# Output sum of the second token tile in three pieces, and two projections copied out of PSUM bank by bank

## The reference, cut to what matters

```python
def hybrid_layer(x, ...):
    h = rms_norm(x, g_pre) * (1 + scale) + shift
    qkv_dn, z_dn, beta_logit, a_logit, qkv_mb, z_mb, merge_logit = split(h @ w_in)
    qkv_dn = silu(causal_depthwise_conv(qkv_dn, conv_w))      # dq, dk, dv in the kernel
    ...                                                       # gated delta rule, 4 heads of 128
    o_mb = moba_attention(q_mb, k_mb, v_mb)                   # bq, bk, bv in the kernel
    ...
    mixed = (gate_dn * y_dn + gate_mb * y_mb) @ w_out         # "out" in the kernel
    return x + gate * rms_norm(mixed, g_post)
```

## Time and profile before

| | us |
|---|---|
| median of 3 runs | 895.02 |
| profiled execution, its own time | 895.32 |
| its span (first to last instruction) | 893.5 |
| PE busy | 884.4 |
| DVE busy | 652.2 |
| ACT busy | 498.4 |

### The profile page before, as it was taken

How to read it: one execution, slowest core, us unless ns; L and a number is a source line. 1 busy time by engine, 2 the same in 40 slices (tenths; PEclk the granted TensorE clock), 3 DMA queues, 4 the chain that set the end, 5 groups by cost and what they waited for, 6 DMA issues and landing times.

```text
span 893.5 us, 13339 instructions
## 1 busy us (share of the span) xinstructions
PE 884.4 (99%) x5610; PEld 756.6 (85%) x5610; DVE 652.2 (73%) x790; ACT 498.4 (56%) x676; POOL 31.1 (3%) x25
## 2 busy tenths in 40 slices
PE   8999999999999999999999999999999999999997
PEld 7889888888888888888888888888879998888885
DVE  6999656569777767699567977777668895556655
ACT  6875556465444454766566544445558774366624
POOL 0000000000000000000000000000000083000000
PEclk9999999999999999999999999999999999999999
DMA  9644444466666664544336666666336344324431
GB/s 357 275 146 179 149 142 142 142 247 222 241 227 240 230 241 167 202 157 161 120 142 255 228 240 230 239 239 235 142 132 244 120 142 143 116 101 155 137 129 47
DMA packets 24155, 165.40 MB, mean 185 GB/s; under 512 B 2688, under 2 KB 2944, under 8 KB 4896
## 3 DMA queue, kind: packets, MB, share of 16 engines
q1 hardware_dynamic: 22608, 159.73, 48.9%
q0 software_dynamic: 1056, 4.34, 1.3%
q10 hardware_dynamic: 432, 0.49, 0.2%
HBM read 163.50 MB, written 1.05 MB: 184 GB/s over the span
## 4 chain that ended last, share of the span: by engine, by line
PE 91%; DVE 5%; ACT 2%; DMA 1%; issue 1%; DVEq 0%; SPq 0%; ACTq 0%
PE acc L633 30%; PE lin L594 11%; PE lin L615 6%; PE lin L622 6%; PE lin L599 6%; PE lin L616 6%; PE lin L573 3%; PE lin L581 3%; PE lin L574 3%; DVE w_lo L1889 2%; PE acc L841 1%; PE acc L725 1%; PE acc L726 1%; DVE arena L2342 1%; PE acc L735 1%; PE lin L678 1%
## 5 line engine op out<-in xcount | busy, mean ns | idle before, releaser
L1889 DVE TENSOR_TENSOR w_lo<-raw,w_hi 128x2048 fp32r<-128x2048 f32 x137 | 318.4, 2336 | 127.7 <-ACT w_hi L1384 127.1
L1384 ACT CAST w_hi<-raw 128x2048 fp32r<-128x2048 f32 x137 | 259.6, 1907 | 138.0 <-DMA raw<-in_weights 86.0
L633 PE MATMUL acc<-w_hi,f_hi 128*128 128x512 f32 x288 | 113.1, 393 | 0.0
L633 PE MATMUL acc<-w_hi,f_lo 128*128 128x512 f32 x288 | 112.4, 390 | 0.0
L615 PE MATMUL lin<-w_hi,h_both 128*128 128x512 f32 x272 | 109.4, 402 | 0.2
L594 PE MATMUL lin<-h_both,w_hi 128*128 128x512 f32 x448 | 106.7, 390 | 0.0
L616 PE MATMUL lin<-w_hi,h_both 128*128 128x512 f32 x272 | 106.3, 391 | 0.0
L594 PEld LDWEIGHTS lin<-h_both,w_hi 128*128 128x128 f32 x448 | 83.2, 188 | 16.7
L633 PE MATMUL acc<-w_lo,f_hi 128*128 128x512 f32 x288 | 78.9, 389 | 0.0
L622 PE MATMUL lin<-w_lo,h_both 128*128 128x512 f32 x272 | 68.1, 390 | 0.2 <-DVE w_lo L1889 0.2
L573 PE MATMUL lin<-h_both,w_hi 128*128 128x256 f32 x272 | 67.3, 287 | 0.0
(11 more groups left out here) (372 smaller groups left out, 1225.7 us busy)
## 6 DMA issues: line engine op xcount, KB each, us to landing
raw<-in_weights SPq DMA_DIRECT2D x149, 1024.0 KB, 4.8
rowbuf<-in_rows POOLq DMA_DIRECT2D x6, 512.0 KB, 4.0
x<-in_x_in SPq DMA_DIRECT2D x2, 512.0 KB, 4.5
raw<-in_weights SPq DMA_DIRECT2D x2, 512.0 KB, 7.3
arena<-in_const_even POOLq DMA_DIRECT2D x1, 1024.0 KB, 11.6
out<-x SPq DMA_DIRECT2D x3, 256.0 KB, 2.1
cst<-in_const SPq DMA_DIRECT2D x1, 580.0 KB, 10.4
out<-x ACTq DMA_DIRECT2D x1, 256.0 KB, 2.1
```

The costliest lines, as they stand in the source:

```text
L633: return pe.matmul(acc[:, at:at + 512], part_of(2 * j + k)[i][:, t * P:(t + 1) * P], w[:, k * 1024 + c * 512:k * 1024 + (c + 1) * 512], st ...
L1384: act.copy(w_hi[:, o % SPLIT, :], raw[:, j % RAW, :]).then_inc(hi_done, 1)
L1889: dve.tensor_tensor(w_lo[:, j % RAW, :], r, hi.bitcast(F32), ALU.subtract).then_inc(tile_split, 1)
```

## The change

1. The second token tile of `out` is summed in three pieces instead of two: columns 0 to 511 in the third bank of `acc`, 512 to 767 in the fourth, 768 to 1023 in the first bank of the pair that `y2a` has left. For the last two pieces each matmul has 256 columns. Squares, gain, update of x and stores follow the pieces; the last two stores have 128 KB each, one from SP, the last from ACT.
2. `dv` is copied out in two copies of 512 columns. The first stands in ACT's list behind the exponentials and ahead of `conv_silu` of q, and waits for the first tile of `dv`; the second stands where the whole copy stood.
3. `bk` is copied out in two copies of 512 columns. The wait for `qg_ready` moves from behind the cast of the second `bv` tile to ahead of it; both copies stand behind the cast.

```diff
+        def last_piece(i):
+            at, width = ((0, 512), (512, 256), (768, 256))[i]
+            return (acc[:, D + at:D + at + width] if i < 2 else pair("y2a")[:, 0:width]), at, width
...
+            for i in range(2):
+                _, at, width = last_piece(i)
+                sp.wait_ge(x_done, done + 3 + i)
+                sp.dma_start(out[0, P:T, at:at + width], x[:, 1, at:at + width]).then_inc(s_out, 16)
+            sp.wait_ge(s_out, 16 * 5)
...
+            def second_tile(n, piece):
+                o, at, width = last_piece(piece)
+                hi = high_tile(FIRST["out"] + n)
+                for k in range(2):
+                    w = slice(k * D + at, k * D + at + width)
+                    for i in range(2):
+                        pe.matmul(o, chunk(2 * n + k)[i][:, P:T], hi[:, w], start=n == 0 and k == 0 and i == 0, stop=False)
+                lo = low_tile(FIRST["out"] + n)
+                for k in range(2):
+                    w = slice(k * D + at, k * D + at + width)
+                    mm = pe.matmul(o, chunk(2 * n + k)[0][:, P:T], lo[:, w], start=False, stop=n == 3 and k == 1)
+                return mm
...
+            for piece in range(3):
+                for n in range(2, 4):
+                    mm = second_tile(n, piece)
+                    if piece == 2:
                         mm.then_inc(tile_used, 1)
+                if piece < 2:
+                    mm.then_inc(acc_done, 1)
...
+            def half_out(name, i, dst):
+                act.wait_ge(tile_used, ORDINAL[FIRST[name] + i] + 1)
+                ins = act.copy(dst[:, i * 512:(i + 1) * 512], pair(name)[:, i * 512:(i + 1) * 512])
+                if i == 1:
+                    ins.then_inc(freed(name), 1)
...
             act.activation(srow(4), srow(2), ACT.Exp).then_inc(erow_ready, 1)
+            half_out("dv", 0, at("pre", 1024, 2048))
             conv_silu(S_AT["q"])
...
             load_exp()
-            copy_out("dv", at("pre", 1024, 2048), splits=False)
+            half_out("dv", 1, at("pre", 1024, 2048))
             split_until(LAST["dv"] + 1)
...
                 if l == 2:
+                    act.wait_ge(qg_ready, 1)
                     split_until(LAST["bq"] + 4)
-                    act.wait_ge(qg_ready, 1)
-                    copy_out("bk", at("bk"), splits=False)
+                    half_out("bk", 0, at("bk"))
+                    half_out("bk", 1, at("bk"))
...
+                after(ss_ready)
+                piece_gain(0)
+                after(ss_ready)
+                link(dve.tensor_scalar(stat[:, 5:6], stat[:, 2:3], stat[:, 3:4], EPS * D, ALU.add, ALU.add))
+                piece_gain(1)
+                after(ss_ready)
+                dve.tensor_tensor(stat[:, 17:18], stat[:, 5:6], stat[:, 4:5], ALU.add).then_inc(ms_ready, 1)
+                piece_gain(2)
+                root_of(1)
+                for i in range(3):
+                    _, at, width = last_piece(i)
+                    part = x[:, 1, at:at + width]
+                    dve.scalar_tensor_tensor(part, arena[:, 6144 + D + at:6144 + D + at + width], stat[:, 9:10], part,
+                                             ALU.mult, ALU.add).then_inc(x_done, 1)
```

More of the change, by code:

```diff
@@ L499, in _ @@
                 sp.dma_start(raw[:, n % RAW, :], weights[n]).then_inc(loaded[n % RAW], 16)
[L500 to L507, removed]
+            done = 4 * (len(SUMS) - 1)
+            for c in range(2):
+                sp.wait_ge(x_done, done + c + 1)
+                sp.dma_start(out[0, 0:P, c * 512:(c + 1) * 512], x[:, 0, c * 512:(c + 1) * 512]).then_inc(s_out, 16)
+            for i in range(2):
[3 more added lines that the diff above has]
+            sp.wait_ge(s_out, 16 * 5)
         @block.gpsimd
@@ L1344, in _ @@
                     mm.then_inc(half_done, 1)
[L1346 to L1349, removed]
-                        mm.then_inc(tile_used, 1)
[L1351 to L1361, removed]
+            def second_tile(n, piece):
[10 more added lines that the diff above has]
+                return mm
+            for n in range(2):
+                row_products(FIRST["out"] + n, n, 0, range(2), chunk, n == 0, False)
+            after(mix_ready)
+            transposes(["y2b"], y_mix, 4)
+            for n in range(2):
+                for piece in range(3):
+                    mm = second_tile(n, piece)
+                mm.then_inc(tile_used, 1)
+            for c in range(2):
+                for n in range(2, 4):
+                    mm = row_products(FIRST["out"] + n, n, 0, (c,), chunk, False, n == 3)
+                mm.then_inc(acc_done, 1)
+            for piece in range(3):
+                for n in range(2, 4):
+                    mm = second_tile(n, piece)
+                    if piece == 2:
+                        mm.then_inc(tile_used, 1)
+                if piece < 2:
+                    mm.then_inc(acc_done, 1)
         @block.scalar
@@ L1417, in last_residual @@
                 split_until(LAST[name] + 2)
[L1418 to L1421, removed]
+                for c in range(2):
+                    sum_squares(name, 0, c)
+                tile_root(0)
+                for i in range(3):
+                    if i < 2:
+                        act.wait_ge(acc_done, 3 * SUMS.index(name) + 3 + i)
+                    else:
+                        act.wait_ge(tile_used, ORDINAL[LAST[name]])
+                    src, at, width = last_piece(i)
+                    act.activation(arena[:, 4096 + D + at:4096 + D + at + width], src, ACT.Square,
+                                   accum_out=stat[:, 2 + i:3 + i]).then_inc(ss_ready, 1)
+                tile_root(1)
             def boundary(name, names, gain, bias=None):
@@ L1848, in _ @@
             last_residual("out")
-            act.wait_ge(x_done, 4 * len(SUMS))
-            act.dma_start(out[0, P:T, 512:D], x[:, 1, 512:D]).then_inc(s_out, 16)
+            act.wait_ge(x_done, 4 * len(SUMS) + 1)
+            act.dma_start(out[0, P:T, 768:D], x[:, 1, 768:D]).then_inc(s_out, 16)
         @block.vector
@@ L1950, in last_residual, with piece_gain @@
                 split_until(LAST[name] + 2)
[L1951 to L1955, removed]
+                after(ss_ready)
+                row_gain(0, 0, row)
+                tile_root(0, lambda: row_gain(0, 1, row))
+                updated(0)
+                def piece_gain(i):
+                    src, at, width = last_piece(i)
+                    link(dve.tensor_tensor(arena[:, 6144 + D + at:6144 + D + at + width], src, row[:, at:at + width], ALU.mult))
+                after(ss_ready)
[3 more added lines that the diff above has]
+                piece_gain(1)
+                after(ss_ready)
+                dve.tensor_tensor(stat[:, 17:18], stat[:, 5:6], stat[:, 4:5], ALU.add).then_inc(ms_ready, 1)
+                piece_gain(2)
+                root_of(1)
+                for i in range(3):
+                    _, at, width = last_piece(i)
+                    part = x[:, 1, at:at + width]
+                    dve.scalar_tensor_tensor(part, arena[:, 6144 + D + at:6144 + D + at + width], stat[:, 9:10], part,
+                                             ALU.mult, ALU.add).then_inc(x_done, 1)
             def boundary(name, names, gain, bias=None):
```

## The result

The changed kernel takes 896.31 us (median of 22 runs, 896.07 to 897.91) against 895.08 us for the kernel before beside it (22 runs, 894.9 to 895.48). The ratio is 1.0016, 95% interval [1.001, 1.0022]: 1.2 us more, inside the 0.2% that the prediction took as its bound for a change that can't be told, though with this many runs it can. Of the 22 executions 18 took 896.07 to 896.79 us and four 897.67 to 897.91, so the means lie 1.46 us apart and not 1.23 (896.59 and 895.13); what sets such a group apart stands with the experiment "Both halves of dv late". The profiled execution took 896.28 us, with a span of 894.5: 1.0 us more than the span before.

A forecast was written before the change was run, and what follows sets the result against it. PE was taken as the bound, busy for 884.4 of 893.5 us. `bk` +1.46, pieces +0.29 and tail -0.44 gave +1.31 us on the median 895.02, predicted as 896.4 us; 8-in-10 range 894.6 to 897.2.

The forecast's parts named there:

- dv, first half: ACT's early `dv` copy delays table load and Silus; square of q 0.71 us late, 0.52 us cover left, cost nothing.
- Rival B: Late Silu of q reaches PE and the delay is paid again in `bk`'s stall: 897.2 us, chance 0.08.
- dv, second half: PE's 0.24 us gap ahead of `dbeta` closes, `qg_ready` comes at about 736.72; gain lasts until PE's next wait.
- bk: Cast waits for `qg_ready`, copies follow it, so PE starts `bv` 1.46 us later; bounds -0.1 to +1.8.
- The pieces on PE: Second token tile of `out`: 24 matmuls of 512 columns become 48 of 256, +0.29 us; bounds 0 to +0.5.
- Behind the last matmul: Shorter square, gain product and last store: store issued 0.34 us sooner, tail -0.44 us in all; bounds -0.7 and 0.
- Nothing gives the time back: After 740 PE stands still only for moments, in chains begun by its own results, so the +1.46 us stays.
- Rival A: `qg_ready` comes ahead of 734.6, DVE being 2.2 us earlier, so the wait costs nothing: 894.7 us, chance 0.13.
- C: DVE's queue and the level loop slip too, holding PE up once more by 1 to 2 us: 898 us, chance 0.07.
- D: Stores are cheap: all as forecast, but tail at -0.7 and pieces at 0.06 us: 895.9 us, chance 0.12.

The follow-up runs named there:

- Both halves of dv late: Changed kernel with the first half copy of `dv` moved down to right ahead of the second: 896.39 us, ratio 1.0014 against the kernel before.
- the version that the runs point to: Changed kernel with the `qg_ready` wait behind the cast again and both `dv` halves where the whole copy stood: 894.58 us, ratio 0.9993 against before.

## Why the prediction was right

896.4 was predicted, 896.31 measured. By its steps:

The mechanism that decides, the cast between `qg_ready` and the copies, was forecast and is shown. That the number came within 0.1 us is in part luck, as the terms below show: traced, they make 1.0 us and not 1.31, and on the two profiled executions (895.32 and 896.28) the difference is 0.96.

*dv, first half.* The load moved behind the copy, the Silus went to 698.37 (698.34 predicted), the square ends at 700.80 (700.77), PE comes at 701.3. The cost was nothing, and holding ACT for some 1.5 us more cost PE what the cover didn't take up, 0.94 us. Rival B had the right place. Its delay is paid once, not nearly twice as I priced it.

*dv, second half.* The gap ahead of `dbeta` closed, DVE's product starts at 735.96 (736.04), and all of it is swallowed at `bv`.

*bk.* The cast starts at 736.67 (736.75), the copies end at 739.55 (739.65), `bv` starts 1.35 us late (1.46). That the cast stands in between, and not the wait, is shown by the two kernels that take it out from there, each 1.7 to 1.8 us faster than after.

*The pieces on PE.* +0.15 us instead of +0.29 (the stage's 16.72 and 16.57). A 256-column matmul takes 0.12 us, as read from `dv`'s rows; part of the error is in the 512-column side: the stage itself paces at 16.57/72 = 0.230, not 0.228. That explains 0.05 of it. The pieces alone had +0.20, so 0.05 is also what this reading varies by between two traces; the rest stays open. By the formula of the Trainium skill (TensorE: Matmul & The Clock Gate, Back-to-back issue gap) the estimate was 0.06; the trace lies between.

*Behind the last matmul.* The square takes 0.48 instead of 0.70, the step of the mean 0.16 instead of 0.21, the gain product 0.34 instead of 0.61, the updates 1.54 as estimated: 0.41 sooner to the store (0.34 predicted). But a store of 128 KB lands no sooner than one of 256 KB, 2.1 us both. The fixed part and bytes over 436 GB/s of the Trainium skill (DMA: Bandwidth & Descriptors, Anatomy of one DMA), by which the prediction's estimate had 0.3 us more, are given there for DMAs from GpSimd's queue. These stores come from SP and ACT, two of them close together, and no run shows a lone one. The sum of the tail is -0.35 instead of -0.44.

*The terms against the span* give +1.0, the sum had +1.31: `bk` is 0.11 less than forecast, the pieces 0.14 less, the tail 0.09 more. The other 0.15 us is lag that goes between 739.6 and 871 (1.35 becomes 1.20). "Nothing gives the time back" was wrong by that much; most of it is gone by 766, where ACT's cast starts 1.24 us later than before, and what gave it back is not traced. The medians differ by 1.23 in one set of runs and by 1.10 in the other. The second price, the halved clock in some executions, stands in no term and no rival; it hardly moves the median and adds 0.2 us to the difference of the means.

*Rival A* was named with the right lever and the wrong reason against it. I held that POOL's work moves along with DVE's and so its price stays. It does move along, but the order in which the two start within 0.03 us decides who is held, and that is worth 0.9 to 1.2 us of `qg_ready`. It does not reach the 2.2 us that would have turned the sign. *C* and *D* did not happen.

## What to carry to other kernels

When a wait is moved ahead of other work on an engine, price the chain from that wait's signal through everything now behind it, up to whoever needs the last of it; the wait's own length says nothing, as 2.2 us of idle ACT cost nothing once the copies came before the cast. Splitting a read-out by bank pays only if the engine reaches the first bank before the second is complete; for `dv` that held at the old place in the list already and closed PE's gap (as a time, `dv`'s part alone is 0.13 us and within the noise), and for `bk` never. Parts of a change that are measured alone need not add up (0.88 - 0.05 - 0.13 = 0.70 against 1.1 to 1.2) if one of them shifts which of two contending engines starts first; and a median over two groups of executions is a price that few of them pay, so look at the single times before adding medians.

## What the runs showed of the hardware that I had not expected

DVE's subtraction of two SBUF tensors (128 x 2048) and POOL's additions (128 x 1020) hold each other up one instruction at a time. Whoever starts first, by 0.003 to 0.03 us in these traces, runs at its own pace, and the other takes about both times together. With POOL first, its first addition takes 2.39 us and DVE's subtraction 4.5. With DVE first, the subtraction takes 2.29 and that addition 4.56, and POOL's three additions take 11.53 us instead of 8.47. DVE's products that read PSUM took 1.21 us in both orders, beside the same additions. If it is first, DVE gains 2.2 us at that subtraction and 1.6 at its next (2.29 instead of 3.88), loses 2.6 again in later products beside POOL (3.02, 2.89 and 1.65 us instead of 2.19, 2.08 and 0.68), and comes out about 1.1 us ahead at `qg_ready`, which is the same size as the whole effect of this change.

A stall of PE can cost more than its length. Behind 1.72 us in which PE stood still, its granted clock was at half, 1.2 instead of 2.4 GHz, for some microseconds in one execution (0.50 between 741 and 743) and at full in others with the same gap. That execution's span is 1.7 us longer, and its mean granted clock is 0.997. The seven executions of the changed kernel at 897.67 to 897.91 us have 0.996 or 0.997 too, and the other 26 have 0.998 or more; so they are most likely of the same kind, though none of them has a trace. It does not follow every such gap: with `bk` copied whole the gap is 1.68 us, and none of 11 executions stands apart. Four kernels in which PE does not wait for the cast ahead of `bv` (the wait behind the cast, copies first, dv's part alone, the version that the runs point to) have no such group in 44 executions between them.
